# Reordered half steps of the S5 stage: outputs and powers behind the next weights, weight splits ahead on ScalarE, Toeplitz transfers on two queues

## The reference, cut to what matters

```python
def s5_bidir(u, disc_f, disc_b, x0_f, x0_b, c_mat=None):
    y_f, x_f = s5_scan(u, disc_f[0], disc_f[1], x0_f, c_mat)
    y_b, x_b = s5_scan(jnp.flip(u, 1), disc_b[0], disc_b[1], x0_b, c_mat)
    y = None if c_mat is None else y_f + jnp.flip(y_b, 1)
    return y, x_f, x_b
# s5_scan: x[t] = lam * x[t-1] + b_bar u[t];  y[t] = Re(c_mat x[t])
...
def merge_branches(y_hy, y_gla, y_s5, gates, w_hy, w_gla, w_s5, w_out):
    g_hy, g_gla, g_s5 = jnp.split(gates.astype(F32), 3, axis=-1)
    m = (jax.nn.sigmoid(g_hy) * (y_hy @ w_hy.astype(F32))
         + jax.nn.sigmoid(g_gla) * (y_gla @ w_gla.astype(F32))
         + jax.nn.sigmoid(g_s5) * (y_s5 @ w_s5.astype(F32)))
    return m @ w_out.astype(F32)
```

## Time and profile before

| | us |
|---|---|
| median of 3 runs | 1557.21 (1552.26 to 1557.29) |
| profiled execution, time | 1555.65 |
| profiled execution, span on the core | 1553.7 |

### The profile page before, as it was taken

The page is one execution under the profiler, slowest core; times in us unless marked ns, Lnnn a source line. Parts: engine busy times, 40 slices in busy tenths (PEclk is TensorE's granted clock), DMA queues, the critical chain, the costliest instruction groups (busy, mean ns, idle before and its releaser), DMA issues.

```text
span 1553.7 us, 15064 instructions
## 1 busy us (share of the span) xinstructions
PE 1279.7 (82%) x5857; PEld 957.7 (62%) x5857; DVE 580.9 (37%) x995; ACT 405.2 (26%) x691; POOL 400.2 (26%) x343
## 2 busy tenths in 40 slices
PE   5579999276975887987759595998949999999994
PEld 1246877255754665766645252765927888888883
DVE  3445225124275566656613858233331000200013
ACT  2364213022133333323222000011151332232312
POOL 2003124003021111202112011122223655556541
PEclk9988989655687978789869898998968999999998
DMA  9320223811011111212133111336241322333211
GB/s 332 110 95 27 82 67 96 139 54 55 27 54 55 43 36 38 75 21 89 48 78 132 41 55 40 136 94 204 82 136 54 109 83 94 109 86 104 93 56 54
DMA packets 137714, 131.48 MB, mean 85 GB/s; under 512 B 12985, under 2 KB 125817, under 8 KB 136620
## 3 DMA queue, kind: packets, MB, share of 16 engines
q1 hardware_dynamic: 121056, 101.91, 22.0%
q0 software_dynamic: 4416, 17.50, 3.2%
q10 hardware_dynamic: 12172, 11.12, 2.9%
HBM read 119.49 MB, written 8.91 MB: 83 GB/s over the span
## 4 chain that ended last, share of the span: by engine, by line
PE 54%; DVE 13%; ACT 3%; issue 3%; POOL 0%; ACTq 0%; DVEq 0%; DMA 0%; POOLq 0%
PE psum L648 45%; DVE buf L2025 2%; PE psum L846 2%; DVE buf L2024 2%; PE psum L802 1%; PE psum L876 1%; PE psum L879 1%; PE psum L798 1%; PE psum L877 1%; DVE buf L2021 1%; PE psum L866 1%; PE psum L677 1%; PE psum L699 1%; DVE buf L1855 1%; DVE buf L1853 1%
## 5 line engine op out<-in xcount | busy, mean ns | idle before, releaser
L1131 POOL TENSOR_TENSOR ring_lo<-buf,ring_hi 128x512 fp32r<-128x512 f32 (+2 forms) x260 | 337.3, 1329 | 832.3 <-ACT ring_hi L1285 832.3
L648 PE MATMUL psum<-hT_hi,ring_hi 128*128 128x512 f32 x744 | 308.3, 414 | 15.9 <-DVE hT_lo L2091 9.5
L648 PE MATMUL psum<-hT_lo,ring_hi 128*128 128x512 f32 x744 | 296.8, 399 | 0.0
L648 PE MATMUL psum<-hT_hi,ring_lo 128*128 128x512 f32 x744 | 296.0, 398 | 0.0
L648 PE MATMUL psum<-buf,buf 128*128 128x512 f32 (+1 forms) x480 | 216.6, 607 | 57.9 <-DVEq L1552 15.6
L1285 ACT ACTIVATE ring_hi<-buf 128x512 fp32r<-128x512 f32 (+2 forms) x260 | 139.8, 609 | 276.6 <-PE psum L648 196.5
L648 PEld LDWEIGHTS psum<-buf,buf 128*128 128x128 f32 x480 | 98.1, 207 | 161.0 <-issue 109.1
L648 PEld LDWEIGHTS psum<-hT_hi,ring_hi 128*128 128x128 f32 x744 | 145.2, 195 | 51.9 <-DVE hT_lo L2091 9.7
L648 PEld LDWEIGHTS psum<-hT_lo,ring_hi 128*128 128x128 f32 x744 | 144.8, 195 | 33.3 <-issue 3.8
L648 PEld LDWEIGHTS psum<-hT_hi,ring_lo 128*128 128x128 f32 x744 | 143.9, 193 | 31.4
L2100 DVE TENSOR_TENSOR buf<-psum,buf 128x512 f32<-128x512 f32 x22 | 15.2, 692 | 224.1 <-PE psum L648 224.1
(11 more groups left out here) (311 smaller groups left out, 1829.8 us busy)
## 6 DMA issues: line engine op xcount, KB each, us to landing
buf<-in_w_in SPq DMA_DIRECT2D x26, 1024.0 KB, 5.3
buf<-in_w_mod SPq DMA_DIRECT2D x24, 1024.0 KB, 5.9
buf<-in_w_ffn_in SPq DMA_DIRECT2D x44, 512.0 KB, 5.1
buf<-in_w_ffn_out SPq DMA_DIRECT2D x8, 1024.0 KB, 5.1
scr_k<-buf POOLq DMA_DIRECT2D x4, 1024.0 KB, 5.5
buf<-scr_k POOLq DMA_DIRECT2D x4, 1024.0 KB, 8.4
buf<-in_w_out SPq DMA_DIRECT2D x4, 1024.0 KB, 7.2
buf<-in_w_ffn_out SPq DMA_DIRECT2D x4, 768.0 KB, 4.5
```

The lines of the kernel that those rows point to most:

```text
L648: ins = nc.tensor.matmul(o, a, b, start=start and n == 0, stop=stop and n == len(pairs) - 1)
L1131: nc.gpsimd.tensor_tensor(ring_lo[:, a:a + n], ring[:, a:a + n], ring_hi[:, h + i * n:h + i * n + n].bitcast(fp32), SUB)\
```

## The change

It has four parts:

1. **Order of the half step.** Before: r(m), [unit A in even half steps], d(m+1), z(m), [y(b-1) in even], x(m), v(m), gen(m+2), unit, k(m), w(m+2). After, even: r(m), d(m+1), z(m), x(m), gen(m+2), unit A, y(b-1), v(m), w(m+2), k(m). After, odd: r(m), d(m+1), unit B, z(m), x(m), v(m), gen(m+2), unit C, w(m+2), k(m).
2. **Splits.** A split that would fall inside a half step of the S5 stage is moved up or down to the beginning of the next half step, ahead of r(m), as long as that is not behind the unit that uses it.
3. **Toeplitz transfers.** SP issues the four of even s, ACT the four of odd s, in its step k(2b+1), after waits for both K copies and for y(b-1).
4. Three waits of DVE on its own earlier results in a shared buffer (WT in v, V9 in r, and a smaller count of V9 in gen).

```diff
         for m in range(2 * NB):
             b, n = divmod(m, 2)
             step("s5_r", b, n)
-            one_beside(n == 0)
             if m + 1 < 2 * NB:
                 step("s5_d", *divmod(m + 1, 2))
+            if n == 1:
+                one_beside()
             step("s5_z", b, n)
-            if n == 0 and b:
-                step("s5_y", b - 1)
             step("s5_x", b, n)
-            step("s5_v", b, n)
+            if n == 1 or b == 0:
+                step("s5_v", b, n)
             if m + 2 < 2 * NB:
                 step("s5_gen", *divmod(m + 2, 2))
             one_beside()
-            step("s5_k", b, n)
+            if n == 0 and b:
+                step("s5_y", b - 1)
+                step("s5_v", b, n)
             if m + 2 < 2 * NB:
                 step("s5_w", *divmod(m + 2, 2))
+            step("s5_k", b, n)
...
+            s5_at = [i for i, st in enumerate(STEPS) if st[0] == "s5_r" and at < i <= first_use[name]]
+            if s5_at and at > s5_first:
+                at = s5_at[0]
...
-                for s in range(T8):
+                for s in range(0, T8, 2):
                     sp.dma_start(Mt[16 * s:16 * s + 16, :, :],
...
                     A(Kall[0:16, :, 0:7, :], o[:, :, 0:7, :], ACT.Copy).then_inc(freed(name), 1)
+                    evacuated(act, f"K{2 * b}")
+                    evacuated(act, name)
+                    if b:
+                        full(act, f"y5{b - 1}")
+                    for s in range(1, T8, 2):
+                        act.dma_start(Mt[16 * s:16 * s + 16, :, :],
+                                      Kall[0:16, :, 7 - s:15 - s, :].rearrange("p g t j -> p g (t j)"))\
+                            .then_inc(S("Mt"), 16)
...
-                    dve.wait_ge(S("V9"), m - 1)
+                    dve.wait_ge(S("V9"), m - 1 if m % 2 or m == 2 else m - 2)
...
+                if n == 0 and 0 < b < NB - 1:
+                    dve.wait_ge(S("WT"), 2 * b + 3)
...
                 dve.wait_ge(S("WT"), min(m + 2, 2 * NB))
+                dve.wait_ge(S("V9"), m)
```

More of the change, by code:

```diff
@@ L571, in hybrid_block @@
         ahead = {}
+        s5_first = STEPS.index(("s5_r", 0, 0))
         for m, name in enumerate(split_order):
```

## The result

The changed kernel takes 1579.83 us (median of 4 runs, 1578.75 to 1583.59), the kernel before 1554.74 us: a ratio of 1.0166, 95% interval 1.0136 to 1.0196. It is slower, as forecast, but by 25 us and not by 10. The profiled execution spans 1576.9 us (1553.7 before).

A forecast was written before the change was run, and what follows sets the result against it. The prediction took a chain mostly through DVE and ACT to bound the S5 stage. 1555.65 - 5.6 (full-clock sum) + 21 (clock) - 3 (start) - 2.7 (end) gave 1565.4, plus 1.6 for the median: 1567 us, range 1547 to 1583.

The forecast's parts named there:

- hole before k: Even half steps: PE empty about 1.7 us between w and k; half clock behind it in half the pairs, 9 us.
- z(2): Start, pair 0: unit A leaves the way of d(1) and z(0); 3 us gained, from 6 gained to 3 lost.
- from z(14) to the end: End: four transfer issues instead of eight per queue let y(7) start earlier; 2.7 us gained, from 1 to 4.
- The prices at full clock: PE pieces on the chain: unit 5.5, merge unit 3.6, y 2.7, d 1.8, k 1.0, z 0.65 us.
- The full-clock sum: Pairs 1 to 6: units 62.2, even-half series 51.3, boundaries 102.45; 216.0 against 221.6 us, 5.6 gained.
- take-overs: Odd half, ahead of the weight copies: sigmoid with table load 1.9 us, hyena copy 0.6, merge nothing.
- The clock: Half clock on the chain between the two z: 21 us lost, bounds nothing to 39.
- The split waits: PE waits for ring_lo ahead of pairs 2 and 6 (6.2 us each) and 4 (5.35); 17.75 us in all.
- The clock did not hold: Rival: fewer PE holes, at most one half-clock stretch on the chain, so the change wins; 1546 us without any; chance 0.16.
- third rival: ACT reaches the splits sooner, so they are no wait; 17.75 us and 9 for restarts go: 1539; chance 0.03.
- Only the three split waits cost clock: Rival: half clock costs 9 us instead of 21; 1555, no difference; chance 0.20.
- Every hole half clock: Rival: every hole of all six pairs brings half clock, 39 us instead of 21; 1585; chance 0.13.

The follow-up runs named there:

- fill_odd_d: Changed kernel with splits at their old places, plus PE matmuls of no use ahead of even k (6) and odd d (8): 1549.45 us, ratio 0.9967.
- after_pool8: Changed kernel with POOL's subtraction for the eight S5 splits over an eighth of the columns (the short subtraction): 1562.15 us, ratio 1.0039.
- fill_split: Changed kernel with 14 PE matmuls of no use ahead of each of the three waits for ring_lo: 1582.34 us, ratio 1.0177.
- old_splits: Changed kernel with the splits back at their old places, new order and two transfer queues kept: 1569.58 us, ratio 1.0089.
- one_queue: Changed kernel with all eight Toeplitz transfers on SP's queue again: 1572.25 us, ratio 1.0107.
- before_twoq: Kernel before the change with the Toeplitz transfers on two queues and nothing else: 1552.97 us, ratio 0.9981.

## Why the prediction was half right

*Direction and structure: right.* The hole before k is 1.86 us in pair 2 (1.7 forecast) and y stands straight behind A. z(2) comes 1.9 us sooner (3 forecast), and from z(14) to the end the kernel is 3.6 us shorter, 2.2 of them up to the start of y(7) (2.7 forecast). Between the two z, 28.8 us were lost where the forecast had a loss of 15.4 (216.0 + 21 against 221.6). Nearly all of the error is there.

*The prices at full clock: right, where nothing else stood in the way.* The forecast for pair 1 without a split wait is A + B 11, 8.55 and 13.85, 33.4 us. In fill_odd_d it takes 33.45 (x at 546.51 and 579.96). Five of the twelve half steps there are within 0.1 us of the forecast.

*The full-clock sum: the step that failed.* It priced every step of DVE as if POOL stood still, and put POOL's effect on DVE at nothing, without a reason: the earlier trace rows has POOL's 5.26 us, and I laid them beside PE and ACT only. With the waits as measured the sum is 216.0 - 0.65. At the 0.24 us for each us at half clock that fill_odd_d gives, the 90 us of the changed kernel cost 22 (an estimate, since the last 22 us at half clock were never taken away). That makes 237.4; the trace has 250.4. So 13 us are missing. The even half steps, from one z to the next, show where:

| even half step of pair | 1 | 2 | 3 | 4 | 5 | 6 |
|---|---|---|---|---|---|---|
| forecast at full clock, split wait as measured | 19.6 | 24.9 | 17.7 | 23.9 | 19.6 | 25.0 |
| changed kernel | 25.8 | 28.3 | 23.9 | 31.4 | 20.6 | 27.5 |
| A, y, k, d, B, z longer than at full clock | 2.9 | 3.4 | 3.8 | 5.4 | 1.7 | 2.5 |
| after_pool8 | 22.5 | 23.1 | 21.2 | 29.3 | 22.4 | 23.2 |

The third row is the length of PE's pieces in the changed kernel less their shortest in these traces (a unit 5.7 us, a merge unit 3.6, y 2.8, k 1.0, d 2.0, z 0.6). In pairs 2, 5 and 6 it covers what the half step has over the forecast. In pairs 1 and 3 some 3 us are left in each, and these are the 3 us that POOL adds to gen, for after_pool8 takes 3.3 and 2.7 us away there. In pair 4 the stores of y hold d for 2.3 us. In the odd half steps d and z are 11.0 us longer than at full clock, and their sum is 8.1 us over the forecast. So by this reading, of one trace, the 35 us over the full-clock sum are some 27 of clock, 6 of POOL and 2 of stores: beside the 22 of the first estimate, the missing 13 are POOL, the stores and some 5 us more of clock. The slowed scan of pair 6 cost nothing; it lay beside unit B.

The take-overs are part of it. The sum had them beside the chain in the even half, but they stand ahead of v on DVE (v 3.8 us behind y in pair 1), they free w's bank (waits of 4.0 and 4.1 us), and they stand behind gen. That is how a slow gen gets onto the chain.

In fill_odd_d the sum is 198.25 (no split waits) and 5 for the clock that is left, against 219.6: 16 are missing. There POOL falls on v: it takes 4.5 us in half step 8 and 5.2 in half step 12, both between y and k, and 5.1 in half step 11, ahead of gen; the x before that takes 1.95 us instead of 0.95, and the scans ahead of z(6) and z(14) 3.1 instead of 1.1. All of these lie on the chain of that trace, and they come to 13 us.

The Trainium skill has the rule for this (SBUF — State Buffer, section "SBUF: two separate sides"): DVE and GpSimd share one pair of ports under an exclusive lock, and a DVE operation with two SBUF inputs and a GpSimd one that reads SBUF block each other for a whole instruction. The rows agree: one of POOL's four subtractions in pair 2 takes 1.27 to 1.70 us, a DVE product of two SBUF operands there 1.74 us instead of 0.68, and one with a PSUM operand 0.42 us, as without POOL. I did not weigh it, and it was the rule that spoke against the change.

*The clock: near as a sum, and in part by luck.* I took 21 us: 9 for restarts behind the split waits, 9 behind the hole before k, 3 for the other boundaries. The two estimates above are 22 and 27. Unit A behind the three waits is some 6 us longer than at full clock, so the first 9 were too many. The other stretches cost 16 to 21 us and not 12, since d is 1.1 to 1.7 us longer than at full clock in nine of the twelve half steps. The errors cancel in part.

*The split waits: right as waits (17.1 us), not as a price.* In place, the short subtraction is worth 17.7 us, of which 11 are these waits. Moving the splits gives 10, and POOL then falls on v.

*The rivals.* The clock did not hold, and the splits do wait. (By its own terms the third rival comes to 1540 and not 1539.) *Only the three split waits cost clock* is wrong: filling them brought no time, and most half clock lies elsewhere. The Trainium skill's section on idle gaps (TensorE: Matmul & The Clock Gate, "HAM oscillation — how this bites in real kernels") holds that idle gaps that are long enough throttle the engine again. The units behind the long waits agree (7.40 to 8.15 us against 5.78 in fill_split). But filling the long waits moved no time, and filling the mostly shorter holes ahead of k and the odd d (1.6 to 4.9 us in old_splits) gave 20 us. *Every hole half clock* (1585) was nearest in time, but with 22 to 27 us of clock, not 39.

*Two queues.* ACT is held 2.97 us ahead of the split where I took 2.3. one_queue puts the price at 7.5 us in the changed kernel, with what it shifts on POOL in it, and before_twoq at a gain of 1.9 in the old order. By their totals the parts are: order +17.8 (1.0114), then the second queue -3.1 (old_splits, intervals overlap), then the late splits +10.2. The same splits gave 8 us in the old order, so a part's sign hangs on what it stands beside.

*What stays open.* The division of the 13 us is read from one trace and confirmed by a run only for POOL's 6 us in pairs 1 and 3. The edits do not add up (fillers are worth 20.1 us with old splits and 2.9 with late ones). Fillers ahead of k and of the odd d were never run apart. Why late splits help the old order was not tested by itself. A POOL that starts behind gen was not tried.

## What to carry to other kernels

Before moving work on an engine, list what the engines beside it do at the new time: an instruction moved under another engine's long one can take two to five times as long, and no list of its own engine shows that. When a reorder puts PE's short pieces in series, ask which of its holes will now be followed by chain work at half clock, and price them all: the mean clock fell only from 0.85 to 0.82, and by the estimates above half clock cost 22 to 27 us. Filling a hole with matmuls of no use is a cheap test for it, but only where the hole is: look in the trace for the half step before choosing.

## What the runs showed of the hardware

- POOL's subtraction and DVE's work on two SBUF operands slow each other. DVE: scan 1.10 to 5.24 us, a product of 512 columns 0.68 to 1.74, of 576 columns 0.76 to 1.8; POOL: 5.26 to 6.48 us. A DVE product with one operand in PSUM is not slowed: 0.42 us for 256 columns, under POOL (584.10) and alone (612.39). Twenty-three such rows lie wholly under POOL in the traces, at 0.40 to 0.42 us.
- With fillers in the three split waits the half clock moved: unit A behind the first went from 7.40 to 5.78 us, k and d behind the next hole from 1.05 and 3.35 to 1.88 and 3.73, and the length stayed (250.4 and 250.2).
- Matmuls of no use in PE's holes raised the mean clock of the stretch from 0.81 to 0.95, and the kernel was 20 us faster for them.
- Four transfers of Kall hold ACT 2.79 us and SP 2.50; eight stores of y hold ACT 3.87.
